# 64 unused bytes per partition ahead of a group of SBUF buffers, in a kernel of two transformer blocks

## The reference

```
h = x + 0.5 * swiglu(rmsnorm(x))                  # feed-forward 1, 1024 -> 2816 -> 1024
h = h + mixer1(rmsnorm(h))                        # sparse and banded attention, two gated branches
h = h + 0.5 * swiglu(rmsnorm(h))                  # feed-forward 2, 1024 -> 2816 -> 1024
x = rmsnorm(h)
mod = silu(c) @ ada_w + ada_b                     # shifts, scales and gates of the second block
proj = (rmsnorm(x) * (1 + sc1) + sh1) @ w_in      # second mixer: q, f, i, g of 512, u of 512
mixed = concat(hgrn2(q, f, i, g), s5(u)) @ w_out  # two recurrences
x = x + gt1 * mixed
x = x + gt2 * peer(rmsnorm(x) * (1 + sc2) + sh2)  # 16384 experts, 8 heads, top 16 each
out = rmsnorm(x)
```

## Time and profile before

| | us |
|---|---|
| median of 3 runs | 2732.63 |
| lowest and highest of them | 2727.27, 2735.01 |
| the profiled execution, its own time | 2734.05 |
| its span, first to last instruction | 2732.2 |
| TensorE matmuls busy in the span | 2642.7 (97%) |
| VectorE busy | 1945.4 (71%) |
| GpSimd busy | 1304.8 (48%) |
| ScalarE busy | 1065.1 (39%) |

### The profile page before, as it was taken

One profiled execution on the slowest core, in us unless ns is written; L12 is line 12 of the kernel. 1 busy time (PEld: TensorE's weight loads), 2 busy tenths in 40 slices (PEclk: granted clock), 3 DMA queues, 4 the chain that ended last, 5 costly groups with the idle time before them and its releaser, 6 DMA issues. The chain is left out here.

```text
span 2732.2 us, 37663 instructions
## 1 busy us (share of the span) xinstructions
PE 2642.7 (97%) x13717; PEld 2229.7 (82%) x13717; DVE 1945.4 (71%) x3096; ACT 1065.1 (39%) x1703; POOL 1304.8 (48%) x622
## 2 busy tenths in 40 slices
PE   8999999999999999999999999998999899999997
PEld 6888887655788887878787799998999878888886
DVE  5445242687854446589777288798999788898998
ACT  4322321455233223342224233344666634444443
POOL 4444452211444444454134367773232367777774
PEclk9999999999999999999999999999999999999999
DMA  5444342111334444332012255566999999999995
GB/s 194 146 141 147 105 167 64 51 59 66 112 122 148 145 146 146 107 108 70 16 55 87 85 170 164 169 225 257 392 389 386 381 359 387 386 387 383 385 392 199
DMA packets 176704, 539.31 MB, mean 197 GB/s; under 512 B 14416, under 2 KB 80080, under 8 KB 154448
## 3 DMA queue, kind: packets, MB, share of 16 engines
q1 hardware_dynamic: 87920, 306.23, 33.4%
q0 software_dynamic: 18432, 134.23, 12.3%
q10 hardware_dynamic: 70240, 97.46, 10.1%
HBM read 482.28 MB, written 55.57 MB: 197 GB/s over the span
## 5 line engine op out<-in xcount | busy, mean ns | idle before, releaser
L358 POOL TENSOR_TENSOR ring_low<-ring,ring_high 128x1024 fp32r<-128x1024 f32 x323 | 800.2, 2478 | 977.9 <-ACT ring_high L318 973.3
L318 ACT ACTIVATE ring_high<-ring 128x1024 fp32r<-128x1024 f32 x354 | 374.1, 1057 | 637.0 <-PE ps L415 485.7
L413 PE MATMUL ps<-u,ring_high 128*128 128x512 f32 (+1 forms) x1504 | 566.5, 377 | 19.8 <-DVE u L520 10.0
L415 PE MATMUL ps<-u,ring_low 128*128 128x512 f32 (+1 forms) x1504 | 560.3, 373 | 0.0
L414 PE MATMUL ps<-u,ring_high 128*128 128x512 f32 (+1 forms) x1504 | 560.2, 373 | 0.0
L358 POOL TENSOR_TENSOR ring_low_more<-ring,ring_high_more 128x1024 fp32r<-128x1024 f32 x103 | 260.9, 2536 | 160.9 <-ACT ring_high_more L318 160.7
L413 PEld LDWEIGHTS ps<-u,ring_high 128*128 128x128 f32 x1504 | 284.3, 189 | 64.0 <-POOL ring_low L641 9.9
L414 PEld LDWEIGHTS ps<-u,ring_high 128*128 128x128 f32 x1504 | 284.5, 189 | 40.3 <-issue 1.4
L415 PEld LDWEIGHTS ps<-u,ring_low 128*128 128x128 f32 x1504 | 284.1, 189 | 39.7
L2868 POOL DMA_INDIRECT fetched_rows<-in_peer_uv,fetch_index x128 | 155.6, 1216 | 181.7 <-DVE ps L2888 138.1
L3495 DVE TENSOR_TENSOR expert_product<-group_acts,group_weights 128x384 f32<-128x384 f32 x128 | 166.5, 1301 | 57.3 <-issue 39.3
(11 more groups left out here) (476 smaller groups left out, 5299.0 us busy)
## 6 DMA issues: line engine op xcount, KB each, us to landing
ring<-in_peer_u SPq DMA_DIRECT2D x128, 512.0 KB, 4.4
ring<-in_peer_uv SPq DMA_DIRECT2D x128, 512.0 KB, 8.3
ring<-in_ffn_gu SPq DMA_DIRECT2D x88, 512.0 KB, 3.5
ada_weights<-in_ada_w SPq DMA_DIRECT2D x48, 512.0 KB, 4.1
ring<-in_ffn_down SPq DMA_DIRECT2D x48, 512.0 KB, 3.5
expert_acts<-kept_acts ACTq DMA_DIRECT2D x128, 192.0 KB, 4.8
expert_weights<-weight_stage ACTq DMA_DIRECT2D x24, 1024.0 KB, 8.0
group_acts<-expert_acts ACTq DMA_DIRECT2D x15, 1536.0 KB, 11.1
```

The lines of the kernel that those rows point to most:

```text
L318: act.activation(k.highs[p], k.ring[:, s], ACT.Copy).then_inc(k.high_ready[p].sem, 1)
L358: pool.tensor_tensor(k.lows[p], k.ring[:, s], k.highs[p].bitcast(F32), ALU.subtract)\
L413: pe.matmul(out, k.highs[p][:, w], high, start=first, stop=False)
L415: last = pe.matmul(out, k.lows[p][:, w], high, start=False, stop=final)
```

## The change

One buffer that nothing reads or writes is opened after `shift_bias`: 16 floats, 64 bytes per partition. The base of what `mixer2` opens goes from 113344 to 113408, which is 886 times 128.

More of the change, by code:

```diff
@@ L3584, in build @@
             k.bias = k.sbuf("shift_bias", [P, 4 * SLOTS], ctx=dense)
+            k.sbuf("line_pad", [P, SLOTS * 4], ctx=dense)
             mixer2(k, later, follows)
```

## The result

| us | before | changed |
|---|---|---|
| median (21 runs each) | 2732.37 | 2736.73 |
| lowest, highest | 2727.27, 2738.32 | 2730.27, 2744.10 |
| profiled execution, own time / span | 2734.05 / 2732.2 | 2735.15 / 2733.3 |

The account below looks back on a forecast made before the run. TensorE was taken to bound the large products; 1.2 us in the down product and 1.3 in the products with v make 2.5 us less, from 2732.63 to 2730.1, said as 2730.0 us; range 2722 to 2737.

Parts of the forecast that it names:

- The reading that decided: ffn_hid and v, 64 bytes past a multiple of 128, run 7.1 ns per triple slower than buffers at multiples of 128.
- first rival: Slower pace of ffn_hid and v has another shared cause, like distance from ring_high, and stays: 2732.6 us; chance 0.15.
- Steps 1 and 2: Down product of feed-forward 2, 1.2 us less; products with v (w_in_2, w_out_2), 1.3 us less; each triple 7.1 ns shorter.
- The share on the path: Matmul savings that shorten the run: 1.2 of 1.25 us in the down product, 1.3 of 1.31 with v.
- step 1: Down product of feed-forward 2: 176 triples x 7.1 ns = 1.25 us, 1.2 taken, between 1.08 and 1.25.
- Steps 3, 4 and 5: Gate and up products of feed-forward 2; S5 and HGRN2 (range -2.7 to +0.1 us); expert stage: zero each.
- The rule of the 16-byte lines: Contiguous accesses within 16-byte SBUF lines run at full bandwidth; both starts are multiples of 16, so the sum would be zero.
- the clock rival: One more low-clock stretch, some 13 us, over the products with w_in_2 or w_out_2 costs 4.8 us: 2734.9; chance 0.12.

Follow-up runs that it names:

- e1: Unused buffer of 448 bytes instead of the changed kernel's 64, giving distance 0 from the weights; ratio 1.0001 [0.9989, 1.0012] to the kernel before.
- e5: Unused buffer of 192 bytes instead of the changed kernel's 64, giving distance 0 from the weights; ratio 1.0001 [0.9988, 1.0014] to the kernel before.
- e3: Kernel before with every buffer from the weight ring on moved up 64 bytes, distances between weights and activations kept; ratio 1.0001 [0.9989, 1.0013].
- e4: Unused buffer of 256 bytes instead of the changed kernel's 64, giving the distance of the kernel before; one run, 2728.82 us.

## Why the prediction was wrong

**The reading that decided.** "So the slower triple goes with the alignment of the moving operand" is the step that failed. The measured 680.0 and 687.1 ns were right: the means over the whole stages are 680.6 and 687.2, 6.6 ns apart, and come back in every kernel at these distances. The inference had two values of one cause beside two values of another: the buffers 64 bytes past a multiple of 128 were also the ones at distance 64 from the weights, and those at multiples of 128 were all at distance 0. A shift of 64 to the next multiple of 128 could go to either distance 0 or 128, and went to 128, where a matmul takes 232.4 ns instead of 229.0. The prediction named this confusion in its first rival ("the distance from the weights in `ring_high`"), gave it 0.15, and had it leave the pace where it was. It should have worked out the distance after the change; the starts that it had were enough for that.

**Steps 1 and 2**, 1.2 and 1.3 us less, had the wrong sign. Pace: +10.0 ns on 176 triples and +10 to +11 on 192 (698.6 ns a triple on `v`), where -7.1 was forecast. On the path: +1.1 us in the down stage, and in that with `w_in_2` some 0.5 to 0.8 us that the pace explains, the rest of its 0.7 to 1.5 being the clock's. Nothing shows in that with `w_out_2`.

**The share on the path** was too high in step 1 as well. It took at most 0.17 us back for waits, by three chunks; e1 and e5 have the pace that was forecast, and the down stage gains 0.6 to 0.8 us instead of 1.2, since the waits for `ring_low` grow from 4.0 to 4.5 us. In the product with `w_in_2` the lengths, 109.1 and 109.2 us, are 0.6 to 0.7 under before and 0.1 to 0.2 over e3 and e4, of a forecast of 120 x 7.1 ns = 0.9 less; with the clock's part taken off as above it is a gain of 0.1 to 0.4. Over the whole stretch they gain 0.9 of the forecast 2.5 us. Both kernels have a ratio of 1.0001; their intervals begin at 0.9989 and 0.9988, so that neither no gain nor the 2.5 us of the forecast is excluded.

**Steps 3, 4 and 5**, nothing, were right: `u` and the expert stage keep 389 ns, VectorE and ScalarE keep 687 and 632, L2211 keeps 275, S5 lasts 120.7 us for 120.6.

**The rule of the 16-byte lines** (the Trainium skill, "SBUF — State Buffer", "Door 1: The DMA port swizzle"), weighed as one that gives no change, doesn't tell this case: all starts in the table are multiples of 16 bytes, and a matmul takes 227.0, 229.0, 232.4 or 233.3 ns.

**The clock.** The changed kernel's trace has a stretch that the earlier trace rows had not, in the first products with `v`:

```profile
1195.00:1199.00 4.00, 3.71 (x9) 2.96 (x10) 4.00 (x4) 3.09 (x5) 0.00 (x0) 0.57 0.39 131
```

By itself this is not the clock rival come true. e3 and e4, as fast as before, have it as well (clock 0.73 and 0.88 from 1195 to 1200 us), and there and here the waits for `ring_low` behind it shrink to 0.9 us, from the 3.1 to 3.6 of before, e1 and e5, which lack it: the first 104 triples take no longer with it (91.8 us in e3 and e4) than without it (92.1 in before). What the clock does cost is in triples 105 to 112, 0.2 us against before and 0.8 against e3 and e4. Whether the change has a part in that is not shown, since before differs from e3 and e4 there by 0.6 us at one distance. The rival's price was too low: it took the lengths of records (394 and 628 ns, 37% lost), while the cost is in the starts, 687 ns a triple against 1280, 46% lost. A stretch of 13 us over these products would cost 6.0 us by that, not 4.8.

## What to carry to other kernels

Where an unbroken chain of fast-format matmuls sets the time, work out the distance from the weight tile to the moving operand, modulo 256 bytes, and make it 0; alignment of the one to 128 alone says nothing. Two groups of buffers that differ in a property are no evidence for it while they differ in a second; before trusting it, put the address after the change into each of the candidate rules. And read a pace by starts, then see from the waits of the stage how much of it can arrive at the end. Before comparing the lengths of two stages, see how much of each ran at the low clock.

## What the runs showed of the hardware

- In an unbroken chain a 128x512 matmul of the fast format takes 227.0 ns start to start at distance 0, 229.0 at 64, 232.4 at 128 and 233.3 at the others measured, 2.8% more than at 0. With the weights 64 bytes further (e2), which slows most large products by up to this, the median is 2761.71 against 2732.98 us, 1.0114 [1.0090, 1.0137].
- The plain float32 matmuls of 128 columns stay at 275 ns under the change, and there weights and moving operands moved together, so no run separates the two.
- After a block at another distance the pace takes ten matmuls to settle (e2, 232 ns and then 227).
- At a granted clock of 0.50 a triple on `v` takes 1280 ns, at 1.00 it takes 687.
- 64 unused bytes cost 4.4 us [2.2, 6.3] of 2732, in 368 triples.
